# NSA attention of one core in steps of two items: scores of both, values of the step two back, then the turns with the filling products around them

## The reference, cut to what matters

```python
def block_fn(args):
    qb, q_blk, g_blk = args
    t = qb * Q_BLOCK + jnp.arange(Q_BLOCK)
    s_c = jnp.einsum('bgrqd,bgnd->bgrqn', q_blk, k_cmp)
    p_c = masked_softmax(s_c, cmp_end[None, :] <= t[:, None])
    o_c = jnp.einsum('bgrqn,bgnd->bgrqd', p_c, v_cmp)
    ...
    s_s = jnp.einsum('bgrqd,bgqnd->bgrqn', q_blk, ks_g)
    p_s = masked_softmax(s_s, tok_ok[:, :, None])
    o_s = jnp.einsum('bgrqn,bgqnd->bgrqd', p_s, vs_g)
    s_w = jnp.einsum('bgrqd,bgnd->bgrqn', q_blk, kwb)
    p_w = masked_softmax(s_w, wmask)
    o_w = jnp.einsum('bgrqn,bgnd->bgrqd', p_w, vwb)
    return g_blk[..., 0:1] * o_c + g_blk[..., 1:2] * o_s + g_blk[..., 2:3] * o_w
...
y = jnp.concatenate([ya, yb], axis=-1) @ w_out
x = x + y
```

## Time and profile before

| | |
|---|---|
| median of 3 runs | 1741.76 us |
| the profiled execution's own time | 1738.36 us |
| its span in the trace | 1735.2 us |
| TensorE busy | 1686.4 us, 97% |
| VectorE busy | 854.8 us, 49% |
| ScalarE busy | 380.5 us, 22% |
| GpSimd busy | 210.8 us, 12% |
| DMA, share of 16 engines (the SyncE queue) | 41.1% |

### The profile page before, as it was taken

The page is one execution under the profiler, slowest core; times in us unless marked ns, Lnnn a source line. Parts: engine busy times, 40 slices in busy tenths (PEclk is TensorE's granted clock), DMA queues, the critical chain, the costliest instruction groups (busy, mean ns, idle before and its releaser), DMA issues.

```text
span 1735.2 us, 19720 instructions
## 1 busy us (share of the span) xinstructions
PE 1686.4 (97%) x7592; PEld 984.2 (57%) x7592; DVE 854.8 (49%) x1486; ACT 380.5 (22%) x681; POOL 210.8 (12%) x280
## 2 busy tenths in 40 slices
PE   7999999999899999999999999999999999999999
PEld 3887876775433333333334447567865554577664
DVE  3755742454523232323325345766755654686663
ACT  1112210001000000000003102231144433454530
POOL 1233410001000000000001000000224430000000
PEclk9999999999899999999999999999999999999999
DMA  7313122234699999999995022312320021121201
GB/s 286 115 61 122 49 71 87 103 146 191 252 408 427 426 427 426 427 426 428 423 427 213 32 81 111 99 55 100 127 98 1 1 73 49 69 78 49 98 1 48
DMA packets 27872, 308.61 MB, mean 178 GB/s; under 512 B 4415, under 2 KB 4703, under 8 KB 10368
## 3 DMA queue, kind: packets, MB, share of 16 engines
q1 hardware_dynamic: 21312, 289.21, 41.1%
q0 software_dynamic: 6464, 18.10, 3.0%
HBM read 306.57 MB, written 4.19 MB: 179 GB/s over the span
## 4 chain that ended last, share of the span: by engine, by line
PE 91%; DVE 3%; DMA 3%; issue 1%; POOL 1%; ACT 0%; SPq 0%; DVEq 0%; ACTq 0%
PE ps L410 87%; PE ps L413 4%; DMA arena<-in_w 2%; DVE arena L1168 1%; DMA arena<-in_rows 1%; DVE arena L1179 1%; DMA wring<-in_dense 0%; DVE arena L1264 0%; POOL small L2726 0%; ACT arena L2295 0%; DVE small L1183 0%; DVE HT L1195 0%; DVE arena L1195 0%; DVE H L1168 0%; DVE wring L1168 0%
## 5 line engine op out<-in xcount | busy, mean ns | idle before, releaser
L410 PE MATMUL ps<-arena 128*64 128x512 f32 (+13 forms) x2384 | 516.9, 398 | 4.4 <-ACT arena L2295 2.1
L410 PE MATMUL ps<-wring,arena 128*64 128x512 f32 (+2 forms) x1136 | 396.4, 579 | 2.5 <-ACT arena L2295 1.6
L410 PE MATMUL ps<-wring,HT 128*128 128x512 f32 (+1 forms) x1040 | 364.7, 503 | 5.2 <-ACT HT L2295 1.9
L1168 DVE TENSOR_TENSOR arena<-ps,arena 128x512 f32<-128x512 f32 (+1 forms) x197 | 134.8, 684 | 463.6 <-PE ps L410 306.0
L410 PEld LDWEIGHTS ps<-arena 128*64 128x64 f32 (+4 forms) x2384 | 232.7, 154 | 222.9 <-issue 211.2
L410 PEld LDWEIGHTS ps<-wring,HT 128*128 128x128 f32 x1040 | 194.8, 192 | 145.0 <-issue 128.9
L2295 ACT ACTIVATE arena<-ps 128x512 f32<-128x512 f32 (+4 forms) x161 | 86.5, 537 | 609.4 <-PE ps L413 306.3
L410 PEld LDWEIGHTS ps<-wring,arena 128*64 128x64 f32 (+1 forms) x1136 | 147.9, 154 | 122.1 <-issue 118.7
L410 PE MATMUL ps<-HT,wring 128*128 128x512 f32 (+2 forms) x528 | 192.7, 530 | 0.0
L410 PE MATMUL ps<-wring 128*128 128x256 f32 x816 | 185.2, 381 | 0.0
L1168 DVE TENSOR_TENSOR H<-ps,H 128x512 f32<-128x512 f32 x182 | 125.8, 691 | 99.0 <-PE ps L410 90.2
(11 more groups left out here) (109 smaller groups left out, 963.8 us busy)
## 6 DMA issues: line engine op xcount, KB each, us to landing
wring<-in_w SPq DMA_DIRECT2D x48, 2048.0 KB, 20.6
wring<-in_dense SPq DMA_DIRECT2D x39, 2048.0 KB, 8.4
arena<-in_w SPq DMA_DIRECT2D x36, 2048.0 KB, 18.1
HT<-in_w SPq DMA_DIRECT2D x12, 2048.0 KB, 17.5
arena<-in_rows POOLq DMA_DIRECT2D x33, 256.0 KB, 5.0
H<-in_x SPq DMA_DIRECT2D x4, 512.0 KB, 3.8
arena<-in_relb POOLq DMA_DIRECT2D x8, 256.0 KB, 8.1
n_scratch<-arena POOLq DMA_DIRECT2D x4, 512.0 KB, 3.3
```

The source lines that it names most:

```text
L410: return nc.tensor.matmul(o, l, r, start=start, stop=stop, skip_group_check=True)
L1168: done(nc.vector.tensor_tensor(o, a, b, op), tell)
```

## The change

The items are taken by twos (`STEPS`, 18 steps). In step i TensorE does the scores of both items, then both values of step i - 2, then, for each item of step i - 1, its slot's filling and its turns. VectorE does the lows of both items (the gating of a finished head pair between them), the weighing of a compressed item in the same step, and then for each item of step i - 1 the filling's part and the copy. Scores get four banks (4 to 7), the turns keep two (2, 3), the fillings have one (1). The probability tiles become eight: the two new ones lie in `xw`, which is free by then. The quota becomes 1.5 pieces a step of two items, with 1.0 ahead.

```diff
-        pD = [nq[:, 512 * i:512 * i + 512] for i in range(4)] + [sq[:, 512 * i:512 * i + 512] for i in range(2)]
+        pD = [nq[:, 512 * i:512 * i + 512] for i in range(4)] + [sq[:, 512 * i:512 * i + 512] for i in range(2)] + \
+            [x[:, 0:512] for x in xw]
...
+        STEPS = [ITEMS[i:i + 2] for i in range(0, NIT, 2)]
+        NSD = len(STEPS)
...
-                               lambda g: {"y1": 1, "e0": 2, "e1": 1}[g[0]], 0.8, NIT + 3, 2.0)
+                               lambda g: {"y1": 1, "e0": 2, "e1": 1}[g[0]], 1.5, NSD + 2, 1.0)
+
+        def items_at(i):
+
+            return STEPS[i] if 0 <= i < NSD else []
...
             def softmax_d(piece):
-                scores, turns, out_, filler = Ring(banks[5:]), Ring(banks[3:5]), Ring(banks[0:1]), Ring(banks[1:3])
+                scores, turns, out_, filler = Ring(banks[4:]), Ring(banks[2:4]), Ring(banks[0:1]), Ring(banks[1:2])
...
-                for i in range(NIT + 3):
-                    if i < NIT:
-                        score(ITEMS[i])
-                    filling(2 * i)
-                    if 0 <= i - 2 < NIT:
-                        turn_probs(ITEMS[i - 2])
-                    filling(2 * i + 1)
-                    if 0 <= i - 3 < NIT:
-                        values(ITEMS[i - 3])
-                filling(2 * (NIT + 3))
+                for i in range(NSD + 2):
+                    for it in items_at(i):
+                        score(it)
+                    for it in items_at(i - 2):
+                        values(it)
+                    for n, it in enumerate(items_at(i - 1) or (None, None)):
+                        filling(2 * i + n)
+                        if it:
+                            turn_probs(it)
+                filling(2 * (NSD + 2))
...
-                            if x >= 6:
-                                full("pt", "D", x - 6)
+                            if x >= 8:
+                                full("pt", "D", x - 8)
...
-                for i in range(NIT + 3):
-                    if i < NIT:
-                        lows(ITEMS[i])
-                    if 0 <= i - 1 < NIT and ITEMS[i - 1]["kind"] == 0:
-                        weigh(ITEMS[i - 1]["hh"])
-                    for g, p in FILL_D[2 * i]:
-                        piece(g, p)
-                    if i < 4:
-                        silu_z(i)
-                    if 0 <= i - 2 < NIT and ITEMS[i - 2]["kind"]:
-                        probs("D", ITEMS[i - 2]["x"], ITEMS[i - 2]["nk"], ptD)
-                    for g, p in FILL_D[2 * i + 1]:
-                        piece(g, p)
-                    if 0 <= i - 3 < NIT and ITEMS[i - 3]["last"]:
-                        hh = ITEMS[i - 3]["hh"]
-                        f = full("yT2", hh)
-                        tt(HT[:, 4 + hh, :], f.ap, zsT[:, hh, :], MUL, f)
+                for i in range(NSD + 2):
+                    for n, it in enumerate(items_at(i) or (None, None)):
+                        if it:
+                            lows(it)
+                        if n == 0:
+                            for was in items_at(i - 2):
+                                if was["last"]:
+                                    f = full("yT2", was["hh"])
+                                    tt(HT[:, 4 + was["hh"], :], f.ap, zsT[:, was["hh"], :], MUL, f)
+                    for it in items_at(i):
+                        if it["kind"] == 0:
+                            weigh(it["hh"])
+                    if i < 2:
+                        silu_z(2 * i)
+                        silu_z(2 * i + 1)
+                    for n, it in enumerate(items_at(i - 1) or (None, None)):
+                        for g, p in FILL_D[2 * i + n]:
+                            piece(g, p)
+                        if it and it["kind"]:
+                            probs("D", it["x"], it["nk"], ptD)
...
```

More of the change, by code:

```diff
@@ L584, in turn_probs @@
                         for c in range(it["q"] + 1):
-                            ins = tr(f.ap[:, c * 128:c * 128 + 128], pD[x % 6][:, c * 128:c * 128 + 128])
+                            ins = tr(f.ap[:, c * 128:c * 128 + 128], pD[x % 8][:, c * 128:c * 128 + 128])
                         ins.then_inc(f.full, 1)
@@ L2017, in piece @@
                         h_add(g[1], g[2], full(*g))
-                for i in range(NIT + 3):
-                    if i < NIT:
-                        lows(ITEMS[i])
-                    if 0 <= i - 1 < NIT and ITEMS[i - 1]["kind"] == 0:
-                        weigh(ITEMS[i - 1]["hh"])
-                    for g, p in FILL_D[2 * i]:
-                        piece(g, p)
-                    if i < 4:
-                        silu_z(i)
-                    if 0 <= i - 2 < NIT and ITEMS[i - 2]["kind"]:
-                        probs("D", ITEMS[i - 2]["x"], ITEMS[i - 2]["nk"], ptD)
-                    for g, p in FILL_D[2 * i + 1]:
-                        piece(g, p)
-                    if 0 <= i - 3 < NIT and ITEMS[i - 3]["last"]:
-                        hh = ITEMS[i - 3]["hh"]
-                        f = full("yT2", hh)
-                        tt(HT[:, 4 + hh, :], f.ap, zsT[:, hh, :], MUL, f)
-                for g, p in FILL_D[2 * (NIT + 3)]:
+                for i in range(NSD + 2):
[18 more added lines that the diff above has]
+                            probs("D", it["x"], it["nk"], ptD)
+                for g, p in FILL_D[2 * (NSD + 2)]:
                     piece(g, p)
@@ L2568, in piece @@
                         copy(HT[:, 0:4, g[1] * 128:g[1] * 128 + 128], f.ap.rearrange("p (k t) -> p k t", k=4), f)
-                for i in range(NIT + 3):
-                    it = ITEMS[i] if i < NIT else None
-                    if it and it["kind"] == 0:
-                        freed(("skc", it["hh"], 1))
-                        p = pC[it["hh"] % 2][:, :, :, 0:31]
-                        act(p, p, ACT.Exp, "ce")
-                    elif it:
+                for i in range(NSD + 2):
+                    for it in items_at(i):
+                        if it["kind"] == 0:
+                            freed(("skc", it["hh"], 1))
+                            p = pC[it["hh"] % 2][:, :, :, 0:31]
+                            act(p, p, ACT.Exp, "ce")
+                            continue
                         for x in (it["x"], it["x"] + 1):
                             freed(("sd", x))
-                            p = pD[x % 6][:, 0:it["nk"]]
+                            p = pD[x % 8][:, 0:it["nk"]]
                             act(p, p, ACT.Exp, "ed", scale=-1.0, bias=small[:, 176 + x % 8:177 + x % 8],
                                 accum_out=sums[:, x:x + 1])
-                    for g, p in FILL_D[2 * i]:
-                        piece(g, p)
-                    if i in (3, 4):
-                        a.wait_ge(S("zg"), 2 * i - 4)
-                    if 0 <= i - 2 < NIT:
-                        it = ITEMS[i - 2]
-                        if it["kind"]:
+                    if i in (1, 2):
+                        a.wait_ge(S("zg"), 2 * i)
+                    for n, it in enumerate(items_at(i - 1) or (None, None)):
+                        for g, p in FILL_D[2 * i + n]:
+                            piece(g, p)
+                        if it and it["kind"]:
                             probs("D", it["x"] + 1, it["nk"], ptD)
-                        else:
+                        elif it:
                             f = full("pc", it["hh"])
@@ L2748, in weigh @@
                 for u in range(2):
-                    p, r = P[(x + u) % 6][:, 0:n], rc[:, x + u:x + u + 1]
+                    p, r = P[(x + u) % len(P)][:, 0:n], rc[:, x + u:x + u + 1]
                     if gate:
```

2 lines of the change are left out of this document (1 added, 1 removed).

## The result

The changed kernel takes 1742.03 us (median of 13 runs, 1739.89 to 1746.52), the kernel before 1738.16 us in its 13 runs beside them (1735.36 to 1742.91). The ratio is 1.0025, 95% interval 1.0016 to 1.0034: slower by 3.9 us. That is inside the 0.3% (5.2 us) that the prediction called no change, but the interval leaves out 1, so the change did cost time. The forecast was +3.0 us and 1744.8; the 1744.8 rests on the 1741.76 of the first three runs, which lay high.

What follows compares the result with a forecast made beforehand. TensorE's own instructions were taken to set the stage's pace, with 0.18 us lost at each change of shape. Terms −8.6 + 3.5 + 0 + 6.5 + 1.6 = +3.0 us gave 1744.8 us, range 1737 to 1752.5.

Steps and rivals of the forecast that it cites:

- Fewer changes of shape, −8.6: TensorE in the attention stage: 48 fewer changes of array shape at 0.18 us each, −8.6 us, ends −7.5 and −10.
- some 8 was given as the sign: Profile after the change: TensorE's busy time in the attention stage some 8 us less.
- The start, +3.5: Stage start: one filling bank and two items of lows in front lengthen waits, +3.5 us, ends +2 and +7.
- The clock, 0: Stage start: half clock comes earlier and longer but partly falls into waits, 0 us, ends −1 and +3.4.
- The rival of the falling clock: Attention stage: new pauses make TensorE's clock fall again, at most some 3.2 us each, +9.4, 1751.2 us; chance 0.18.
- The later compressed items, +6.5: Three later compressed steps: TensorE waits for late VectorE at turns and output gating, +6.5 us, ends +2 and +9.
- Products on one bank, +1.6: Products sharing one filling bank wait for additions to H in four places, +1.6 us, ends 0 and +6.
- The rival in which the bank binds at every product: Late VectorE additions to H delay 16 results by 0.5 us each, +9.4, 1751.2 us; chance 0.08.
- The sum: Whole kernel: all terms together give +3.0 us, 1744.8 us from the three-run median 1741.76; no change to be measured, chance 0.54.
- from 5 to about 15: Profile after the change: TensorE's idle time in the attention stage up from 5 to about 15 us.

Runs made afterwards that it cites:

- split pairs: Changed kernel with TensorE's step written as scores a, values a, scores b, values b, 24 more changes of array shape: 1744.48 us, ratio 1.0036.
- late weighing: Changed kernel with VectorE weighing a later compressed item's probabilities at the end of the step, behind copies and additions: 1742.97 us, ratio 1.0029.
- Held values: Changed kernel with the values of a compressed item standing second in its step waiting for the next step: 1739.03 us, ratio 1.0007.
- the interleaved kernel: Changed kernel with VectorE and ScalarE taking the second item's lows and exponentials between the slots, weighing behind its lows' slot: 1738.87 us, ratio 1.0003.
- ScalarE's order alone: Changed kernel with only ScalarE taking the second item's exponentials between the slots, VectorE as in the change: 1741.90 us, ratio 1.0023.
- the copies of y1 first: Changed kernel with ScalarE copying turned y1 before exponentials in the first two steps, VectorE its own before weighing and silu: 1742.63 us, ratio 1.0025.
- both improvements: Changed kernel with second items' lows and exponentials between the slots and second compressed items' values a step later: 1733.80 and 1735.13 us, ratios 0.9973 and 0.9988.

## Why the prediction was right, step by step

- **Fewer changes of shape, −8.6.** The mechanism is shown by the split pairs (0.19 each, 0.18 said), and a block of two items' scores and values costs what was written. The term itself came out as −6.9 and −6.5 in content, beyond the end of −7.5. A change of shape that stands in a pause is counted as idle time and not as content, but that does not explain the missing 1.7 us: the kernel before has three of these (at 1277.58 and 1278.92 in the earlier trace rows, and at 1282.60) and the changed kernel two (the 1.17 us each). 48 changes fewer at 0.14 is what came out, and why it is less than 0.19 stays open. TensorE's busy time in the stage fell by 4.3 and 6.3 us, where some 8 was given as the sign, since half clock adds to it.
- **The start, +3.5.** Said: pauses of 4.0, 0.8, 2.8 and 0.2. Measured: 3.83 and 1.70, the second not at all. The pauses of the start are 5.5 us in sum, 2.2 more than before, for +3.5 in the sum. The second pause goes with the clock: where this fell 1.1 and 1.4 us after the second turn of y1 (late weighing, split pairs), that pause is there, with 0.71 and 0.95 us; where it had fallen before that turn, or fell within 0.3 us of it (the changed kernel, twice), TensorE's own work took longer and the pause is absent. That the filling bank causes the start's waits is wrong as a reading: with it relieved, the wait moved to the next turn.
- **The clock, 0.** 2.6 us more than before were lost at half clock in the first profile, within the end of +3.4, and 0.2 more in the second. The rival of the falling clock, with 0.18, is true in part: a stretch at 0.50 came at 1384.8, behind the pauses of 1.77 and 1.17, in one of two profiles. Five of 13 runs lie some 4 us above the others, most of them with a lower mean clock. Its price of at most 3.2 us a fall was high for the late one (1.7).
- **The later compressed items, +6.5.** Said: 1.3 at a turn behind VectorE's copy, 1.3 twice at the gating, others of 1.3 to 1.8. Measured: 1.25, 1.17 twice, 1.06 and 1.77. That is 6.4 us in sum, 5.8 more than the 0.6 before. One of them was released by ScalarE and one was a product's, not a turn's. Held values show the cause of the two at the gating by removing them; the interleaved kernel removes or shrinks the other three, at the price of two new ones. ScalarE's order alone won nothing.
- **Products on one bank, +1.6.** 0.44 and 0.57 stood at products, 1.0 in sum, and the 1.77 that is counted above. The rival in which the bank binds at every product is out: one bank in the kernel before costs 0.17 us in the later products.
- **The sum.** +3.0 said, +3.9 measured by the medians, +4.2 and +2.9 in the stages of the two profiles. Idle time from 5.9 to 14.4 us (15.1 in the second) against "from 5 to about 15" is the number that carried the verdict. That the sum came so close is in part luck. The terms of waiting add up to +11.6 and idle time grew by 8.5 and 9.2; content fell by 1.7 and 2.1 us less than said, and the clock took 2.6 and 0.2. These errors cancel.

The Trainium skill's sentence on draining at a change of tiling mode ("TensorEngine Tiling (Array Packing)", Key Properties) agrees with the split pairs, 0.19 us for each added change. What the Trainium skill tells of a clock that swings when TensorE cycles through PSUM banks ("TensorE: Matmul & The Clock Gate", A second HAM failure mode: psum-queue depth-cycling) is not shown at work here: with one filling bank in the kernel before, half clock lasted 13.7 us in place of 6.8, but it also varied between two profiles of one kernel, 10.2 and 3.4 us.

## What to carry to other kernels

Pairing work of one array shape paid 0.14 us for each change saved in the whole stage (0.19 when the pairs were split again), but it delivers twice the work at once to the engines behind. Their orders are worth rewriting with TensorE's: each consumer takes one item, then makes the copies that free TensorE's banks, then takes the other. Before moving a bank from one ring to another, ask where TensorE would stand next if that bank were free: at the start and at the weighing the answer was "at the next turn", and nothing was won. Only the held values and the interleaved order of VectorE and ScalarE won time, and with both the paired kernel is 2 to 5 us below the one before.

## What the runs showed that was not expected

- TensorE's clock fell to half for 3.4 us late in the stage in three profiles: at 1384.8 in the changed kernel, 1.5 us after a pause of 1.17 and 12 us after one of 1.77; at 1353.9 with the late weighing, 0.7 us after a pause of 1.88; at 1372.0 with ScalarE alone, in a pause of 3.20. The second profile of the changed kernel has the same late pauses as the first and no late fall; the held values and the copies of y1 first have the 1.77 and no late fall either. So a pause of this size does not bring it with certainty.
- At the start the length at half clock varied from 3.4 to 13.7 us, and between two profiles of the same kernel: 10.2 and 3.4 us with both improvements, one stretch of 10.2 and two of 3.4 in the changed kernel, where the clock came back for 3.4 us between them (1.00 from 1284.5 to 1287.9). A difference of some us at half clock between two kernels' single profiles shows nothing about the kernels.
